# A weight stream loaded in two halves per unit: each 1 MB transfer becomes two of 512 KB

## The reference

```python
for l in range(DEPTH):
    sh_l, sc_l, g_l = jnp.split(jax.nn.silu(c) @ w_mod[l] + b_mod[l], 3, axis=-1)
    sh_c, sc_c, g_c = jnp.split(jax.nn.silu(c_ctx) @ w_mod[l] + b_mod[l], 3, axis=-1)
    hl = xl * (1.0 + sc_l[:, None, :]) + sh_l[:, None, :]
    hc = xc * (1.0 + sc_c) + sh_c
    parts_l = jnp.split(hl @ w_in[l], SPLIT_POINTS, axis=-1)
    ...
    out_l = _mix_output(parts_l, att_l, ...)          # conv, attention, pool, then @ w_out[l]
    xl = _layernorm(ALPHA * xl + g_l[:, None, :] * out_l, ln_g[l], ln_b[l])
```

## Time and profile before

| | |
|---|---|
| median of 3 runs | 2875.14 us (2873.31 to 2875.14) |
| time of the profiled execution | 2876.09 us |
| its span, first to last instruction | 2874.4 us |
| PE busy | 2846.0 us, 99% of the span |
| DVE, ACT busy | 1876.2 us (65%), 1328.1 us (46%) |
| stream queue (q1) | 515.95 MB, 49.1% of 16 DMA engines' time |

### The profile page before, as it was taken

The page is one execution under the profiler, slowest core; times in us unless marked ns, Lnnn a source line. Parts: engine busy times, 40 slices in busy tenths (PEclk is TensorE's granted clock), DMA queues, the critical chain, the costliest instruction groups (busy, mean ns, idle before and its releaser), DMA issues.

```text
span 2874.4 us, 42472 instructions
## 1 busy us (share of the span) xinstructions
PE 2846.0 (99%) x15570; PEld 2384.3 (83%) x15570; DVE 1876.2 (65%) x3394; ACT 1328.1 (46%) x2044; POOL 112.5 (4%) x179
## 2 busy tenths in 40 slices
PE   8999999999999999999999999999999999999998
PEld 6778787777788788888888888888888888888887
DVE  3368686764577636666886666667876556565566
ACT  2343333323332534544556555556656445354445
POOL 0000000101000001111000100000000000000000
PEclk9999999999999999999999999999999999999999
DMA  9954444443365334344445544444555555555555
GB/s 377 361 192 182 164 166 177 162 171 152 152 237 206 117 105 157 136 147 148 171 162 191 191 174 178 171 180 171 183 189 202 191 186 197 190 181 199 188 192 190
DMA packets 78220, 530.66 MB, mean 185 GB/s; under 512 B 9416, under 2 KB 11728, under 8 KB 15472
## 3 DMA queue, kind: packets, MB, share of 16 engines
q1 hardware_dynamic: 73872, 515.95, 49.1%
q0 software_dynamic: 3328, 10.63, 1.1%
q10 hardware_dynamic: 864, 1.95, 0.2%
HBM read 526.37 MB, written 2.12 MB: 184 GB/s over the span
## 4 chain that ended last, share of the span: by engine, by line
PE 96%; DVE 1%; DMA 1%; ACT 1%; issue 1%; POOL 0%; POOLq 0%; ACTq 0%; DVEq 0%; SPq 0%
PE bank L2015 28%; PE bank L2018 14%; PE bank L2005 9%; PE bank L2007 9%; PE bank L2006 9%; PE bank L2425 4%; PE bank L2426 4%; PE bank L2424 4%; PE bank L2051 2%; PE bank L2052 2%; PE bank L2053 2%; PE bank L2234 1%; DMA raw<-stream 1%; PE bank L2193 1%; PE bank L2064 1%; PE bank L2074 1%
## 5 line engine op out<-in xcount | busy, mean ns | idle before, releaser
L1182 DVE TENSOR_TENSOR w_lo<-raw,w_hi 128x1024 fp32r<-128x1024 f32 x784 | 947.2, 1224 | 439.6 <-ACT w_hi L670 437.0
L670 ACT ACTIVATE w_hi<-raw 128x1024 fp32r<-128x1024 f32 x784 | 823.4, 1056 | 651.0 <-DMA raw<-stream 214.8
L2005 PE MATMUL bank<-x,w_hi 128*128 128x512 f32 x1120 | 442.8, 395 | 3.0 <-issue 1.8
L2007 PE MATMUL bank<-x,w_lo 128*128 128x512 f32 x1120 | 436.2, 389 | 0.0
L2006 PE MATMUL bank<-x,w_hi 128*128 128x512 f32 x1120 | 436.1, 389 | 0.0
L683 ACT ACTIVATE z<-bank 128x512 f32<-128x512 f32 x256 | 153.3, 599 | 472.3 <-PE bank L2018 298.2
L2015 PE MATMUL bank<-xs,w_hi 128*128 128x512 f32 x1184 | 303.9, 397 | 0.0
L2005 PEld LDWEIGHTS bank<-x,w_hi 128*128 128x128 f32 x1120 | 210.2, 188 | 70.1 <-issue 26.8
L2015 PE MATMUL bank<-mlp_x,w_hi 128*128 128x512 f32 x1024 | 257.1, 393 | 0.0
L2007 PEld LDWEIGHTS bank<-x,w_lo 128*128 128x128 f32 x1120 | 210.2, 188 | 44.6
L2015 PEld LDWEIGHTS bank<-xs,w_hi 128*128 128x128 f32 x1184 | 213.8, 189 | 40.1 <-DVE xs L1292 1.1
(11 more groups left out here) (353 smaller groups left out, 3590.4 us busy)
## 6 DMA issues: line engine op xcount, KB each, us to landing
raw<-stream SPq DMA_DIRECT2D x488, 1024.0 KB, 4.8
res<-tokens POOLq DMA_DIRECT2D x8, 512.0 KB, 8.9
work<-tokens POOLq DMA_DIRECT2D x16, 256.0 KB, 3.1
res<-cond_rows SPq DMA_DIRECT2D x8, 256.0 KB, 4.2
out<-res SPq DMA_DIRECT2D x8, 256.0 KB, 2.4
gain_sb<-final_gain ACTq DMA_DIRECT2D x1, 1024.0 KB, 6.0
table_sb<-tables ACTq DMA_DIRECT2D x1, 640.0 KB, 3.5
pool_sb<-pool_w POOLq DMA_DIRECT2D x8, 64.0 KB, 2.2
```

The source lines that it names most:

```text
L670: own.inc(act.activation(w_hi[:, 2 * unit.parity + g, :], raw[:, unit.slot, g * HALF:(g + 1) * HALF], ACT.Copy), hi_done, 2 * unit.number ...
L1182: own.inc(dve.tensor_tensor(w_lo[:, n, :], raw[:, unit.slot, g * HALF:(g + 1) * HALF], w_hi[:, n, :].bitcast(F32), ALU.subtract), lo_done, ...
L2005: pe.matmul(bank[:, :], hi, tile(k)[:, 0, :], start=k == 0, stop=False)
L2007: ins = pe.matmul(bank[:, :], lo, tile(k)[:, 0, :], start=False, stop=k == KT - 1)
```

## The change

Every place is transferred as two halves of 512 KB (1024 columns, 4 KB in each partition), each with a semaphore of its own. SP issues the two one after the other. Where the slot was held by a unit, the first half is issued when the first half of that unit has been subtracted (`lo_done` odd), the second when the second has; where it was held by a modulation piece, both wait for the whole piece. The users wait for their own half: ACT before each rounding, PE in the middle of a modulation piece. DVE, where it uses modulation pieces, waits for both halves at once.

```diff
-        raw_full = [sem(f"raw_full{n}") for n in range(RAW_SLOTS)]
+        raw_full = [[sem(f"raw_full{n}_{g}") for g in range(2)] for n in range(RAW_SLOTS)]
...
-            def load(place, slot):
-                sp.dma_start(raw[:, slot, :], stream[place]).then_inc(raw_full[slot], 16)
+            def load_half(place, slot, g):
+                part = slice(g * HALF, (g + 1) * HALF)
+                sp.dma_start(raw[:, slot, part], stream[place, :, part]).then_inc(raw_full[slot][g], 16)
...
-                elif before in weight_at:
-                    sp.wait_ge(lo_done, 2 * weight_at[before] + 2)
-                load(place, place % RAW_SLOTS)
+                for g in range(2):
+                    if before in weight_at:
+                        sp.wait_ge(lo_done, 2 * weight_at[before] + 1 + g)
+                    load_half(place, place % RAW_SLOTS, g)
...
-                    sp.wait_ge(lo_done, 2 * AHEAD + 8 * i + 2 * n + 2)
-                    load(PLACES + RAW_SLOTS + 4 * i + n, (PLACES + n) % RAW_SLOTS)
+                    for g in range(2):
+                        sp.wait_ge(lo_done, 2 * AHEAD + 8 * i + 2 * n + 1 + g)
+                        load_half(PLACES + RAW_SLOTS + 4 * i + n, (PLACES + n) % RAW_SLOTS, g)
...
             def round_half(unit, g):
 
-                if g == 0:
-                    act.wait_ge(raw_full[unit.slot], 16 * (unit.wave + 1))
+                act.wait_ge(raw_full[unit.slot][g], 16 * (unit.wave + 1))
...
             def gate_products(k):
 
                 place, group, q = mod_place(GATED + k), k // 4, k % 4
-                dve.wait_ge(raw_full[place % RAW_SLOTS], 16 * (place // RAW_SLOTS + 1))
+                for g in range(2):
+                    dve.wait_ge(raw_full[place % RAW_SLOTS][g], 16 * (place // RAW_SLOTS + 1))
...
             def mod_early(u):
 
                 place, side = mod_place(u), u % 2
-                pe.wait_ge(raw_full[place % RAW_SLOTS], 16 * (place // RAW_SLOTS + 1))
                 for n in range(KT):
+                    if n % 8 == 0:
+                        pe.wait_ge(raw_full[place % RAW_SLOTS][n // 8], 16 * (place // RAW_SLOTS + 1))
                     rows = slice(SQUARE * (n % 4), SQUARE * (n % 4 + 1))
```

More of the change, by code:

```diff
@@ L533, in _ @@
                 for n in range(RAW_SLOTS):
-                    sp.wait_ge(lo_done, 2 * AHEAD + 8 * i + 2 * n + 2)
-                    load(PLACES + RAW_SLOTS + 4 * i + n, (PLACES + n) % RAW_SLOTS)
+                    for g in range(2):
+                        sp.wait_ge(lo_done, 2 * AHEAD + 8 * i + 2 * n + 1 + g)
+                        load_half(PLACES + RAW_SLOTS + 4 * i + n, (PLACES + n) % RAW_SLOTS, g)
             for n in range(2):
-                sp.wait_ge(lo_done, 2 * (WEIGHTS - 6 + n) + 2)
-                load(MODS + WEIGHTS - 2 + n, (PLACES + n) % RAW_SLOTS)
+                for g in range(2):
+                    sp.wait_ge(lo_done, 2 * (WEIGHTS - 6 + n) + 1 + g)
+                    load_half(MODS + WEIGHTS - 2 + n, (PLACES + n) % RAW_SLOTS, g)
             for t in range(2):
@@ L2060, in mod_product @@
                 window = slice(2 * (SHARE - 1 - group), 2 * (SHARE - 1 - group) + SQUARE)
-                pe.wait_ge(raw_full[place % RAW_SLOTS], 16 * (place // RAW_SLOTS + 1))
                 for j in range(4):
+                    if j % 2 == 0:
+                        pe.wait_ge(raw_full[place % RAW_SLOTS][j // 2], 16 * (place // RAW_SLOTS + 1))
                     rows = slice(SQUARE * j, SQUARE * (j + 1))
```

## The result

| | before | changed |
|---|---|---|
| median | 2874.8 us (11 runs) | 2881.07 us (11 runs, 2878.18 to 2885.08) |
| ratio to before | | 1.0023, 95% interval 1.0015 to 1.0031 |
| time of the profiled execution | 2876.09 us | 2879.03 us |
| its span | 2874.4 us | 2877.4 us |

The kernel became 0.23% slower; one slow run of the kernel before, 3128.71 us, is left out of the ratio. 2873.4 us was forecast, and the result lies above the range's upper end of 2878.5.

The account below looks back on a forecast made before the run. PE was taken to bound the kernel, with DMA a near-bound in the first stage. Gains of 0.78, 0.96 and 0.3 us less a price of 0.34 gave -1.7 from 2875.14, so 2873.4 us, range 2870.0 to 2878.5.

Parts of the forecast that it names:

- Price of the smaller pieces: Stream in first stage: two 4 KB pieces at 167 ns against one 8 KB at 326; +0.34 us, bounds 0 and +4.5.
- the point at which DMA overtakes PE: First stage, two turns: DMA and PE are level at 14.76 / 88 = 168 ns per 4 KB piece.
- DMA becomes the bound in the first stage, mildly: Rival: at 175 ns a piece, +4.5 less 2.0 gives +2.5, 2877.6 us; chance 0.20 together with no effect.
- Start: Second early product: PE's 0.78 us wait for all of place 1 goes, its first half there at about 8.6; gain 0.78.
- Waits in turns 3, 7 and 14: First stage, second piece of a turn: half the product (0.54 us) runs inside PE's wait for the stream; gain 0.96.
- unit 7: Late in first stage: second subtraction ends at 123.1 in place of 124.32, PE's input-tile wait shrinks; gain 0.3.
- sum of the gains: First stage: start 0.78, waits in three turns 0.96 and unit 7 0.3, before the price of +0.34.
- After the first stage: 488 more issues of 0.33 us and second halves about 0.4 us later stay hidden, since PE does not wait there.
- A fixed part paid by each transfer alone: Rival: 2.2 us for each of 38 more transfers in the first stage, +84, 2957 us; chance 0.03.
- the fast rival: Rival: 4 KB pieces let the conditioning vector through up to 1.6 us sooner; -6.2, 2868.9 us; chance 0.08.

Follow-up runs that it names:

- whole_pitch8: Kernel before, whole 1 MB transfers and its waits kept, but 4 KB pieces laid out at a pitch of 8 KB in HBM: 2883.29 us, 1.0026.
- early_halves: Against the kernel before, only the first 40 places (first stage) are transferred as halves, all later ones whole: 2879.55 us, 1.0015.
- halves_contig: Changed kernel with each half laid out as one run of 512 KB in HBM (pitch 4 KB): 2873.70 us, 0.9994 to the kernel before.
- halves_pitch32: Changed kernel with four places side by side, so that a half's pieces lie 32 KB apart: 2872.19 us, 0.9991 to the kernel before.
- late_halves: Against the kernel before, the first 40 places stay whole and all later ones are halves: 2873.72 us, 0.9995.
- few_halves: Against the kernel before, halves only at places 1, 36, 37 and from 40 on, the rest whole: 2875.89 us, 0.9999.
- parts_8k: Kernel before with each place as two transfers of 64 partitions each, pieces still 8 KB, users waiting for both: 3030.54 us, 1.0540.
- halves_wait_both: Changed kernel's transfers, but users wait for both halves and a slot is freed as a whole: 2883.82 us, 1.0031 to the kernel before.

## Why the prediction was wrong

**Price of the smaller pieces: this step failed.** It read the price of a stream piece off the tokens' queue, 167 ns, on the ground that it "moves just such pieces, 4 KB from rows that lie 32 KB apart". Same size, other pitch. At the pitch of 32 KB the stream's own pieces do take 168 ns, at the 8 KB that the change gave them 174, with 172 and 179 in the two windows that the prediction had used. The text named the distance and did not ask whether it mattered. The tokens' own price did not hold either: beside the stream at its new pitch it rose from 169 to 180 ns over 20 to 120 us. Since the point at which DMA overtakes PE was 168 ns, 6 ns decided. DMA became the longer one in the first stage, which is the rival "DMA becomes the bound in the first stage, mildly". That the mechanism is this one and no other part of the change is shown by the pitch alone bringing the loss to whole transfers (whole_pitch8) and by another pitch taking it from the halves.

**The size of the mild bound.** The rival's own formula gives (174 - 168) x 88 x 7 = +3.7 us. Less the 2.0 of gains that makes 2876.8, where 2881.07 was measured. What it left out, in the profile, is the spell at 1.2 GHz behind the 2.12 us wait, 1.6 us. The profiled execution is 2.9 us above that of before, the medians differ by 6.3; other executions of the changed kernel are up to 6 us longer, with a mean granted clock of 0.996 or 0.997 where the profiled one had 0.998. No trace of these executions was taken, but early_halves has the same transfers and waits up to the end of the first stage, and its profiled execution shows how much more the stage can lose: it ended at 152.77 us, 6.5 later than before, with a wait of 2.7 us in the turns and a spell at 0.50 behind it.

```profile
118.50:121.50 3.00, 3.00 (x9) 2.32 (x8) 0.00 (x0) 0.00 (x0) 0.00 (x0) 0.50 1.03 412
...
152.77 0.50 PE L2085 MATMUL bank<-w_hi,x 128*128 128x512 f32 x1 [0.52 <-DVE w_lo L1214]
```

So the loss of this stage varies from execution to execution, and the medians' 6.3 lies within what was seen. That the changed kernel's slower executions lose it in the same way is argued and not shown.

**Start: gain of 0.78.** The conditioning tile did come sooner: the first product starts at 6.22 in place of 7.34. But PE then waits 1.32 for the first half of place 1, and the second product ends at 9.47 + 2.28 = 11.75, where it ended at 10.06 + 1.93 = 11.99. The lead is 0.24 there. I had place 1's first half at 8.6 us by the mean rate of the first stage; it came at 9.47. By the first value product the lead has grown to 1.04 (19.11 in place of 20.15 us), for a reason that the sum had no term for: the products between took less time. The 32 rows of `mod_early(2)`, in two groups, took 0.65 + 1.38 us before and 0.42 + 1.04 now. So a lead of about the size forecast was there, but not by the wait that was to go: that the number agrees is luck.

```profile
17.13 0.65 PE L2074 MATMUL bank<-raw,cond_x 128*32 128x128 f32 x6
...
17.98 1.38 PE L2074 MATMUL bank<-raw,cond_x 128*32 128x128 f32 x26
```

```profile
16.85 0.42 PE L2081 MATMUL bank<-raw,cond_x 128*32 128x128 f32 x6
...
17.28 1.04 PE L2081 MATMUL bank<-raw,cond_x 128*32 128x128 f32 x26
```

**Waits in turns 3, 7 and 14, unit 7.** The wait of turn 14 is gone and that for unit 7 as well (one wait for an input tile in place of two, -0.3 as predicted). That of turn 3 is 0.73 in place of 0.62 although only half a product hangs on it, and turns 5, 9, 11 and 13 wait, where none had: the late stream took these gains back. In halves_contig and halves_pitch32 there are no such waits in the turns, the stage ends 2.6 to 2.8 us sooner than before, and the ratios 0.9994 and 0.9991 would be 1.7 to 2.6 us. But their intervals reach 1.0003 and 1.0000, and late_halves, whose first stage is that of the kernel before, ended it 1.5 us sooner as well:

```profile
144.75 0.50 PE L2087 MATMUL bank<-w_hi,x 128*128 128x512 f32 x1 [0.49 <-DVE w_lo L1216]
```

So the sum of the gains, -2.04, is of the size that a kernel shows whose stream keeps up, but it is not shown beyond the scatter.

**After the first stage, right.** No new wait of PE for a unit; late_halves 0.9995. The 488 more issues and the later second halves are hidden, as said: ACT's waits for the stream from 146 to 2800 us shrank from 213.4 us to 194.1. The issues of the changed kernel, which answer to the earlier trace rows:

```profile
raw<-stream SPq DMA_DIRECT2D x976, 512.0 KB, 4.6
...
cond_sb<-cond ACTq DMA_DIRECT2D x1, 16.0 KB, 4.2
```

**The other rivals.** A fixed part paid by each transfer alone would have been +84 us; 976 transfers at a pitch of 4 or 32 KB are not slower than the 488 of before (0.9994, 0.9991). The size rule of the Trainium skill's page "DMA: Bandwidth & Descriptors", section "Bandwidth", asks for 1 MiB and more; here, on SP's queue and with the DMA engines 95 to 97% busy in the first stage, the runs at 512 KB do not agree with it. What the fast rival built on did happen: the conditioning vector's 16 KB landed after 4.2 us in place of 5.3, and PE's first wait shrank by 1.1. That the queues take turns by pieces is not shown by it. As the text against it said, place 1 must still land, and so most of it became the wait of 1.32.

## What to carry to other kernels

A price read off another queue was good only for the pitch in HBM that it was read at, and not even there once the stream beside it had changed; where a stage has DMA and PE nearly level, a few nanoseconds a piece decide, so measure the new access pattern before trusting a margin of 1%. If a tile is to be loaded in parts, let the host lay each part out as a run of its own: it costs the kernel nothing, and here turned a loss of 0.23% into no loss. And when a stretch gets slower, look for the place where the late stream also lets the granted clock fall.

## What the runs showed of the hardware

A pitch of 8 KB made 4 KB pieces 4 to 7% dearer in the mean (174 to 178 ns against 167 to 168 side by side), 16 KB as dear by the piece but with half the loss, and 12, 24 and 32 KB hardly (168 to 170 ns) and with no loss. The median piece took 159 ns throughout; the price lies in the share of pieces over 250 ns, 5.2 to 5.8% against 1.6 to 2.2. The Trainium skill, "DMA: Bandwidth & Descriptors", section "Latency and other measured facts", reports copies between HBM tensors at row pitches of 512 KiB to 8 MiB, 207 GB/s at 512 KiB and 103 at the largest, where 4 KiB of padding at 4 MiB gave 214, and names aliasing of memory channels as an inference. The runs here agree in that padding by 4 KB cures it (8 to 12 KB, 174 to 169 ns); they differ in that the loss came at a pitch far smaller than these, and went away as the pitch grew to 32 KB.

Transfers that fill 64 of the 128 partitions ran at little more than half the rate: 597 ns for 8 KB in place of 330, and 224 GB/s in both queues, 202 of them in the stream's (20.25 MB in 100 us), with the DMA engines busy throughout. In the Trainium skill, "SBUF — State Buffer", section "Door 1: The DMA port swizzle", 64 neighbouring partitions reach half of the memory's ports, about 218 GB/s; the stream's 202 agrees.

A small transfer on another queue landed sooner beside a stream of 4 KB pieces than beside one of 8 KB in most of these kernels: the conditioning vector's 16 KB took 3.7 to 4.6 us in nine kernels with 4 KB pieces at the start and 5.2 to 5.3 in three with pieces of 8 KB (before, late_halves and, but for three places, few_halves). Two do not fit: whole_pitch8, with 4 KB pieces, took 5.5, and parts_8k, with 8 KB pieces to 64 partitions, 1.6.

After a wait of 2.12 us PE worked at the granted clock of 0.50 for about 3.4 us, which cost nearly as much (1.6 us) as the wait itself. In early_halves the same followed on a wait of 2.7 us; in halves_wait_both no such spell followed on its wait of 2.56 us.
